# A first tile whose row sums move from TensorE to GpSimd, chunk by chunk

## What is computed

```python
x = x + rms_norm(mixed, ln_mix_post)
h2 = rms_norm(x, ln_ffn_pre)
f = (jax.nn.silu(h2 @ w_ffn_gate) * (h2 @ w_ffn_up)) @ w_ffn_down
```

## Time and profile before

| what | value |
|---|---|
| median of 3 runs | 2166.91 us (2163.98 to 2169.29) |
| the profiled execution | 2169.65 us |
| its span | 2167.8 us |
| TensorE busy (matmul) | 2041.6 us, 94% of the span |
| VectorE busy | 762.9 us, 35% |
| GpSimd busy | 621.9 us, 29% |
| ScalarE busy | 507.4 us, 23% |
| mean granted TensorE clock | 0.963 |

### The profile page before, as it was taken

How to read it: one execution, slowest core, us unless ns; L and a number is a source line. 1 busy time by engine, 2 the same in 40 slices (tenths; PEclk the granted TensorE clock), 3 DMA queues, 4 the chain that set the end, 5 groups by cost and what they waited for, 6 DMA issues and landing times. The chain is left out here.

```text
span 2167.8 us, 33107 instructions
## 1 busy us (share of the span) xinstructions
PE 2041.6 (94%) x13732; PEld 1949.5 (90%) x13732; DVE 762.9 (35%) x1440; ACT 507.4 (23%) x922; POOL 621.9 (29%) x506
## 2 busy tenths in 40 slices
PE   7999999976799989999989799999999999998997
PEld 6999989854678879999989799999999999998797
DVE  4104433232778864122231623102212221333623
ACT  4121011133477762010021311110000000001423
POOL 2223200000355444323423123332223323321230
PEclk9999999976899999999999799999999999999999
DMA  6233354124100011111112221111111112113111
GB/s 238 60 90 116 98 217 156 39 107 187 55 2 2 2 46 48 44 44 44 44 49 98 78 78 46 37 53 49 44 44 53 44 37 61 49 31 141 36 37 79
DMA packets 157127, 150.89 MB, mean 70 GB/s; under 512 B 18600, under 2 KB 149234, under 8 KB 154130
## 3 DMA queue, kind: packets, MB, share of 16 engines
q1 hardware_dynamic: 154178, 111.43, 16.7%
q0 software_dynamic: 2304, 33.56, 3.9%
q10 hardware_dynamic: 528, 4.23, 0.5%
HBM read 132.28 MB, written 21.10 MB: 71 GB/s over the span
## 5 line engine op out<-in xcount | busy, mean ns | idle before, releaser
L573 PE MATMUL ffn_acc<-HH,WS 128*128 128x344 f32 x2112 | 395.7, 322 | 8.5 <-DVE HL L505 7.4
L581 POOL CAST WS<-W 128x1024 fp32r<-128x1024 f32 (+2 forms) x125 | 131.7, 1054 | 873.8 <-PE ffn_acc L573 542.4
L573 PEld LDWEIGHTS ffn_acc<-HH,WS 128*128 128x128 f32 x2112 | 345.0, 189 | 8.9 <-issue 7.5
L583 POOL TENSOR_TENSOR WS<-W,WS 128x1024 fp32r<-128x1024 f32 (+2 forms) x125 | 301.6, 2413 | 10.0
L573 PE MATMUL ffn_acc<-HL,WS 128*128 128x344 f32 x1056 | 225.2, 322 | 0.0
L573 PE MATMUL ffn_acc<-AH,WS 128*128 128x344 f32 x1056 | 195.4, 320 | 0.0
L573 PE MATMUL proj_acc<-HH,WS 128*128 128x344 f32 x912 | 174.3, 324 | 7.3 <-DVE HL L505 7.3
L573 PEld LDWEIGHTS ffn_acc<-HL,WS 128*128 128x128 f32 x1056 | 179.8, 190 | 0.0
L573 PEld LDWEIGHTS ffn_acc<-AH,WS 128*128 128x128 f32 x1056 | 171.7, 188 | 0.0
L573 PEld LDWEIGHTS proj_acc<-HH,WS 128*128 128x128 f32 x912 | 149.1, 189 | 8.0 <-issue 6.0
L573 PE MATMUL merge_acc<-HH,WS 128*128 128x344 f32 x768 | 146.8, 323 | 6.8 <-DVE HL L505 6.8
(11 more groups left out here) (412 smaller groups left out, 3389.7 us busy)
## 6 DMA issues: line engine op xcount, KB each, us to landing
W<-in_w_in SPq DMA_DIRECT2D x30, 512.0 KB, 3.9
W<-in_w_ffn_gate SPq DMA_DIRECT2D x22, 512.0 KB, 3.9
W<-in_w_ffn_up SPq DMA_DIRECT2D x22, 512.0 KB, 3.8
W<-in_w_ffn_down SPq DMA_DIRECT2D x16, 384.0 KB, 3.4
W<-in_w_ffn_down SPq DMA_DIRECT2D x16, 320.0 KB, 3.1
kept_x<-Z SPq DMA_DIRECT2D x1, 4128.0 KB, 13.3
Z<-kept_x SPq DMA_DIRECT2D x1, 4128.0 KB, 14.4
kept_x<-Z ACTq DMA_DIRECT2D x1, 4128.0 KB, 11.7
```

The costliest lines, as they stand in the source:

```text
L573: last = k.nc.tensor.matmul(acc[:, s, n, 0:NW], k.WS[:, ws, part, c, :], src[:, c, n * NW:(n + 1) * NW], start=(c == 0 and part == 0 and s ...
L581: k.nc.gpsimd.tensor_copy(k.WS[:, ws, 0, 0:nk, :], w).then_inc(hi_done, 1)
L583: k.nc.gpsimd.tensor_tensor(k.WS[:, ws, 1, 0:nk, :], w, k.WS[:, ws, 0, 0:nk, :].bitcast(F32), ALU.subtract).then_inc(split_done, 1)
```

## The change

GpSimd adds up the squares over the chunks: it copies the first chunk's squares to `k.ssq` and adds those of the other seven, each when ScalarE has made it. TensorE does one set of row sums, over `k.ssq`, behind the last chunk's nine matmuls and the last of these adds. The zeros, their semaphore and the two matmuls with them go. A buffer of squares is free again when GpSimd has added it, where it was free when TensorE had read it. GpSimd's new instructions stand behind the split of the first up weights, and wait for the first root's row sums to have read `k.ssq`.

```diff
                     pool.wait_ge(down_done, d0 + s + 1)
                     split_weights(k, pool, s, s, DC, hi_done, t0 + s, split_done)
+                if t0 == 0:
+                    pool.wait_ge(roots[0].mean, 1)
+                    for c in range(DC):
+                        pool.wait_ge(squared2, c + 1)
+                        if c == 0:
+                            nc.gpsimd.tensor_copy(k.ssq, k.sq[:, 0, :]).then_inc(summed2, 1)
+                        else:
+                            pool.wait_ge(summed2, c)
+                            nc.gpsimd.tensor_tensor(k.ssq, k.ssq, k.sq[:, c % 2, :], ALU.add).then_inc(summed2, 1)
...
             row_spread(k, flat, roots[0].rs).then_inc(spread, 1)
-            pe.wait_ge(zeroed, 1)
-            nc.tensor.matmul(aux[:, 1, 0:9], k.ident[:], zeros, start=True, stop=False)
             pe.wait_ge(split_done, 3)
             for c in range(DC):
                 pe.wait_ge(h.lo_done, c + 1)
                 last = split_tile(k, acc, 0, 0, k.HH, k.HL, c + 1, first=c, more=c < DC - 1)
                 if c == DC - 1:
                     last.then_inc(gate_done, 1)
-                pe.wait_ge(squared2, c + 1)
-                row_sums(k, aux[:, 1, 0:9], k.sq[:, c % 2, :], first=False, last=False).then_inc(summed2, 1)
-            nc.tensor.matmul(aux[:, 1, 0:9], k.ident[:], zeros, start=False, stop=True).then_inc(roots[1].mean, 1)
+            pe.wait_ge(summed2, DC)
+            row_sums(k, aux[:, 1, 0:9], k.ssq).then_inc(roots[1].mean, 1)
             pe.wait_ge(roots[1].rooted, 1)
...
-            nc.vector.memset(zeros, 0.0).then_inc(zeroed, 1)
             roots[0].clear(dve)
```

More of the change, by code:

```diff
@@ L2159, in ffn @@
         aux = st.psum("aux", [P, 2, 512])
-        gate_done, up_done, silu_done, gated, down_done, acc_free, hi_done, split_done, slot_ok, a_hi, a_lo, x_back, scaled, rescaled, spread, mixed, x_new, squared2, summed2, r_copied, spilled, zeroed = st.sems(
-            "gate_done up_done silu_done gated down_done acc_free hi_done split_done slot_ok a_hi a_lo x_back scaled rescaled spread mixed x_new squared2 summed2 r_copied spilled zeroed")
+        gate_done, up_done, silu_done, gated, down_done, acc_free, hi_done, split_done, slot_ok, a_hi, a_lo, x_back, scaled, rescaled, spread, mixed, x_new, squared2, summed2, r_copied, spilled = st.sems(
+            "gate_done up_done silu_done gated down_done acc_free hi_done split_done slot_ok a_hi a_lo x_back scaled rescaled spread mixed x_new squared2 summed2 r_copied spilled")
         done = (gate_done, up_done)
@@ L2167, in ffn @@
         roots = [RowRoot(k, st, "mix"), RowRoot(k, st, "pre")]
-        zeros = k.E[:, 5400:5409]
         flat = acc[:, 1].rearrange("p n w -> p (n w)")[:, 0:N]
```

## The result

The changed kernel takes 2177.13 us (median of 18 runs, 2174.72 to 2181.13), the kernel before in the same rounds 2168.83 (18 runs, 2163.98 to 2175.91). The ratio is 1.0037, 95% interval 1.0030 to 1.0045: slower, by 8.3 us between the medians where 7.1 were forecast. The 1.9 us by which the kernel before is now slower than its first median are not the change's.

A forecast was written before the change was run, and what follows sets the result against it. TensorE was taken as the bound; with VectorE's adds waiting for GpSimd, the last add to x comes 9.8 us later, the tail gives some back: +7.1 us on 2166.91 makes 2174.0 us, range 2169.5 to 2178.5.

The forecast's parts named there:

- The bound, and what is left without the row sums: First tile: TensorE works without a gap; without row sums per chunk, VectorE's undisturbed pace of 3.67 us a chunk is left.
- The port: Loop: VectorE's add to x waits while a GpSimd add reads SBUF; chunk 5.74 us, last add to x 9.8 us later.
- The reaction to the square: Loop: GpSimd starts its add some 0.15 us after ScalarE's square ends, with 0.05 to 0.25 as the ends.
- The tail's terms: Behind the last add to x: low half, nine matmuls, last GpSimd add and row sums; root at 1255.20, was 1248.08.
- TensorE starts 0.15 later and needs 2.72 at half clock: Tail: chunk 7's nine matmuls start 0.15 us after its low half ends at 1248.98 and run to 1251.85.
- 18 row-sum matmuls, 3.24 us: Tail: the single set of row sums takes 3.24 us at the first one's rate, then 0.11 to VectorE.
- Root, spreading, copy and the up tile are as before: Behind the loop: these steps keep their times, so the +7.1 us at the root reaches the end.
- rival 1: Up tile starts at half clock, two matmul groups cost 1.20 us more each: +9.5 us, 2176.4; chance 0.15.
- Rival 2: Clock is full at the tail, so the last nine matmuls and row sums are shorter: +5.4 us, 2172.3; chance 0.13.
- Rival 3: Loop: GpSimd and VectorE's two port users alternate without idle time, 4.87 us a chunk: +1.9 us, 2168.8; chance 0.09.
- The race does not matter: Loop: if GpSimd reacts later than 0.30 us, VectorE's add comes first and the sum is +7.3 us instead.
- The store of x: Store to memory lands at 1260.3, before VectorE needs it at 1261.3, so it costs nothing.

The follow-up runs named there:

- e1: Changed kernel with GpSimd's copy and adds replaced by memsets that read nothing, sum of squares left out: 2161.52 us, ratio 0.9968 to the kernel before.
- e2: Changed kernel with GpSimd adding only 516 of the 1032 columns, the others left out: 2167.25 us, ratio 0.9995 to the kernel before.
- e3: Changed kernel with each GpSimd add also waiting for the same chunk's low half, so it stands beside the scaling: 2171.7 us, ratio 1.0016 to before.
- e8: The changed kernel again, unchanged, for a second profiled execution: 2174.93 us.
- e9: The changed kernel again, unchanged, for a third profiled execution: 2175.11 us.
- e7: Changed kernel with each GpSimd add also waiting for the next chunk's add to x: 2171.85 us, ratio 1.0013 to the kernel before.
- e6: Against the changed kernel, TensorE sums fp32r squares as moving data against ones; no adds of squares, no spreading: 2156.64 us, ratio 0.9934 to before.

## Why the prediction held, and where it was off

- **The bound, and what is left without the row sums.** Right: 3.67 us a chunk, seen plainly in e1.
- **The port.** Right in mechanism and size. Predicted and measured: GpSimd add 2.36 and 2.38; add to x about 3.3 and 3.25; chunk 5.74 and 5.69; end of the last add to x (e(7), less the 1.52 by which the stage is later) 1246.40 and 1246.08. The reaction to the square was taken as 0.15 us and is 0.07. e1 and e2 show that the wait is that of reading and follows the length, e3 that an instruction with a PSUM operand does not take part.
- **The tail's terms.** Two were off and nearly cancel. "TensorE starts 0.15 later and needs 2.72 at half clock" left out that chunk 6's nine matmuls, whose low half comes only 1.4 us before chunk 7's, are still running: from e(7) to the row sums it took 1254.18 - 1247.60 = 6.58, predicted 5.45. "18 row-sum matmuls, 3.24 us" was the half-clock rate; they took 2.01, with 0.11 to VectorE 2.12 in place of 3.35. Together with e(7) -0.3 + 1.1 - 1.2 = -0.4: +6.7 at the root, where +7.1 were worked out. That the tail came out nearly right is luck: two terms of the wrong size, with opposite signs.
- **"Root, spreading, copy and the up tile are as before".** This is the step that does not always hold. In the profiled execution the up tile began at half clock, which is rival 1, priced at 2.4 us beyond the forecast and measured at 2.65; in e8 and e9 it did not. I had argued that the work just ahead of that tile is the same as before. That was so, and yet the clock came out both ways. Against the kernel before, TensorE idles in the loop, 8.12 of 15.10 us busy; but it does so in all three executions of the changed kernel, with the same clock at the same places of the stage. What makes the up tile's clock differ between them was not settled.
- **Rival 2, the clock full at the tail**, half came true: the row sums ran at the full-clock rate, the nine matmuls ahead of them did not. The granted clock of 0.5 named for the loop was 0.61 and 0.58 in its halves; as VectorE bounds the loop, that moved nothing.
- **Rival 3, turns without idle**, did not happen in the changed kernel; e3 (4.83) and e7 (4.55) come to its 4.87 by another order.
- **"The race does not matter"** was a claim about VectorE's add coming ahead of GpSimd's by a late reaction. That order was not made; e3 and e7 shift GpSimd's start by other waits and change the chunk by 0.9 and 1.1 us. I would not write the sentence again.
- **The store of x**, costed at nothing, did cost nothing: VectorE's wait before L2347 ends with the copied root (L2302).

## What to carry to other kernels

Before work goes to an idle GpSimd, count how many of VectorE's instructions there read two SBUF operands: beside such instructions a GpSimd add of 2.38 us cost VectorE 2.02 us, more than the 1.15 of doing it there. If it must be GpSimd, let it start beside an instruction that reads PSUM (e3), or let it come second (e7): the same work then costs 0.9 to 1.1 us less per chunk, though neither of these two kernels came under the time before. And the sum over partitions was cheaper here with the data, rounded for it, moving against ones than with the data as weights: 0.63 against 1.90 us of TensorE per chunk, no add elsewhere, and the result on all partitions (e6).

## What the runs showed of the hardware

- VectorE and GpSimd do not lose the same time by an equal conflict: who comes first by 0.2 us runs in full, the other stands (3.25 for 1.23, or 3.33 for 2.38).
- VectorE's low half starts 0.08 us before the end of the add to x ahead of it, and so is 0.21 us earlier than a GpSimd add that the end of that add releases (e7).
- A RECIPROCAL over 1032 columns takes VectorE 6.60 us, more than five adds of that size; in e6 it cost nothing, as the up tile ran meanwhile.
- GpSimd fills 128 by 1032 elements in 0.96 us (e1); in the changed kernel it copies them in 1.09 (L2212), and an add takes 2.38.
